# Adaptive-norm projections split over four 32-column groups of TensorE's array, in a fused two-layer decoder step

## The reference, cut to what matters

```python
cs = jax.nn.silu(c)                                   # 9 x 1024
for li in range(DEPTH):                               # DEPTH = 2
    mod = cs @ ada_w[li] + ada_b[li]                  # 9 x 3072
    shift, scale, gate = jnp.split(mod, 3, axis=-1)
    h = rmsnorm(x, norm_g[li]) * (1.0 + scale[:, None]) + shift[:, None]
    ...                                               # y = pool_branch(h) or gla_branch(h)
    x = x + gate[:, None] * y
return rmsnorm(x, final_g), ...
```

## Time and profile before

| | |
|---|---|
| median of 3 runs | 1827.49 us (1827.28 to 1830.14) |
| span of the profiled execution (first to last instruction) | 1825.0 us |
| TensorE busy with matmuls | 1747.8 us, 96% of the span |
| VectorE, ScalarE, GpSimd busy | 794.3, 509.7, 403.2 us |
| the 96 matmul records of line 1429 (layer 0's projections) | 592 ns each |
| the 384 records of line 1463 (layer 1's) | 273 ns each |

### The profile page before, as it was taken

The page is one execution under the profiler, slowest core; times in us unless marked ns, Lnnn a source line. Parts: engine busy times, 40 slices in busy tenths (PEclk is TensorE's granted clock), DMA queues, the critical chain, the costliest instruction groups (busy, mean ns, idle before and its releaser), DMA issues.

```text
span 1825.0 us, 26848 instructions
## 1 busy us (share of the span) xinstructions
PE 1747.8 (96%) x10405; PEld 1609.0 (88%) x10405; DVE 794.3 (44%) x1211; ACT 509.7 (28%) x1085; POOL 403.2 (22%) x404
## 2 busy tenths in 40 slices
PE   7899999999999999996999999999999999999997
PEld 4299999999999999994798799997999989999896
DVE  1655345634663466347113362133621336313365
ACT  5511111111111112115315322253222542124422
POOL 1222121212121212113214212142121331123310
PEclk9999999999999999998999999999999999999999
DMA  9222221221122122201111211112111121111212
GB/s 336 88 62 61 70 60 52 61 70 54 59 61 70 51 62 61 70 13 25 42 40 48 87 48 36 47 37 92 53 36 47 36 93 41 47 47 35 87 47 98
DMA packets 145141, 115.17 MB, mean 63 GB/s; under 512 B 5597, under 2 KB 127865, under 8 KB 145026
## 3 DMA queue, kind: packets, MB, share of 16 engines
q1 hardware_dynamic: 143402, 112.86, 19.9%
q10 hardware_dynamic: 1632, 0.65, 0.2%
HBM read 98.95 MB, written 15.00 MB: 62 GB/s over the span
## 4 chain that ended last, share of the span: by engine, by line
PE 89%; DVE 6%; ACT 2%; issue 2%; POOL 1%; ACTq 0%; DVEq 0%; POOLq 0%
PE psA L454 44%; PE psB L454 29%; PE psB L1623 2%; PE psX L1463 2%; PE psB L1573 2%; PE psB L1590 2%; PE psX L1555 1%; PE psX L1612 1%; PE psB L1581 1%; DVE PQ L385 1%; DVE h_lo L376 1%; PE psX L1429 1%; PE psB L351 1%; DVE y_rows L1380 1%; DVE a_hi L525 1%
## 5 line engine op out<-in xcount | busy, mean ns | idle before, releaser
L305 POOL TENSOR_TENSOR w_lo<-stage,w_hi 128x1024 fp32r<-128x1024 f32 x112 | 278.7, 2489 | 1081.9 <-ACT w_hi L300 1081.9
L454 PE MATMUL psA<-h_hi,w_hi 128*128 128x362 f32 (+1 forms) x1152 | 278.0, 350 | 13.0 <-POOL w_lo L305 6.1
L454 PE MATMUL psA<-h_lo,w_hi 128*128 128x362 f32 (+1 forms) x1152 | 256.1, 331 | 0.0
L454 PE MATMUL psA<-h_hi,w_lo 128*128 128x362 f32 (+1 forms) x1152 | 255.0, 330 | 0.0
L454 PEld LDWEIGHTS psA<-h_hi,w_hi 128*128 128x128 f32 x1152 | 199.9, 192 | 58.4 <-issue 51.1
L300 ACT ACTIVATE w_hi<-stage 128x1024 fp32r<-128x1024 f32 x112 | 119.8, 1071 | 314.7 <-PE psB L454 228.2
L454 PEld LDWEIGHTS psA<-h_lo,w_hi 128*128 128x128 f32 x1152 | 203.1, 191 | 0.0
L454 PEld LDWEIGHTS psA<-h_hi,w_lo 128*128 128x128 f32 x1152 | 202.6, 191 | 0.0
L454 PE MATMUL psB<-h_hi,w_hi 128*128 128x362 f32 (+1 forms) x576 | 128.2, 330 | 2.2 <-ACT kT L936 2.2
L454 PE MATMUL psB<-h_lo,w_hi 128*128 128x362 f32 (+1 forms) x576 | 126.3, 327 | 0.0
L454 PE MATMUL psB<-h_hi,w_lo 128*128 128x362 f32 (+1 forms) x576 | 125.9, 327 | 0.0
(11 more groups left out here) (261 smaller groups left out, 2498.8 us busy)
## 6 DMA issues: line engine op xcount, KB each, us to landing
stage<-in_gla_w_in SPq DMA_DIRECT2D x40, 512.0 KB, 3.8
stage<-in_pool_w_in SPq DMA_DIRECT2D x32, 512.0 KB, 4.0
ada_stage<-in_ada_w SPq DMA_DIRECT2D x24, 512.0 KB, 3.8
ada<-in_ada_w SPq DMA_DIRECT2D x4, 2048.0 KB, 21.4
stage<-in_pool_w_out SPq DMA_DIRECT2D x16, 512.0 KB, 3.5
v<-in_state_gla SPq DMA_DIRECT2D x32, 256.0 KB, 2.6
out_new_gla_sample<-v SPq DMA_DIRECT2D x32, 256.0 KB, 2.0
stage<-in_gla_w_out SPq DMA_DIRECT2D x16, 512.0 KB, 3.6
```

The source lines that it names most:

```text
L305: nc.gpsimd.tensor_tensor(w_lo[:, j % 2, :], stage[:, j % 2, :], w_hi[:, j % 2, :].bitcast(f32), ALU.subtract).then_inc(lay.lo_done, 1)
L454: last = nc.tensor.matmul(ps[u][:, t, 0:width], weight(w[:, p, :], k), a[:, k, n0:n0 + width], start=(k == 0 and pas == 0), stop=(k == kt ...
```

## The change

The eight contraction tiles of a projection no longer all go to columns 0 to 8 of the array. Tile k uses column group k % 4, and so writes to PSUM partitions 32(k % 4) to 32(k % 4) + 31; the stationary operand is 32 columns wide, 9 of them the wanted ones, the others those of the next tile, whose results nobody uses. Each group sums two tiles (k and k + 4). ScalarE copies all 128 partitions. The turn is now a matmul with `sel`, a 128 x 9 matrix of zeros and ones, which adds the four partial sums and turns them in one step. GpSimd makes `sel`, and clears `csT`, whose last 23 columns are read but not written otherwise.

```diff
+CG = 32
-        csT = sb("csT", [P, KD, NC_])
-        mod_row = sb("mod_row", [NC_, P], stack=early)
+        mod_row = sb("mod_row", [P, P], stack=early)
+        csT = sb("csT", [P, KD * NC_ + CG - NC_], stack=early)
+        sel = sb("sel", [P, NC_], stack=early)
...
             link(pool.memset(eps[:], EPS))
+            link(pool.memset(csT[:], 0.0))
+            link(pool.memset(sel[:], 0.0))
+            for j in range(4):
+                link(pool.affine_select(out=sel[:], in_=sel[:], compare_op=ALU.not_equal, fill=1.0, base=-CG * j,
+                                        pattern=[[-1, NC_]], channel_multiplier=1))
             pool.memset(gs_tmp[:], 0.0).then_inc(consts_ready, 1)
...
-                nc.scalar.activation(mod_rows[:, i * 512:(i + 1) * 512], X[i % 2][0:NC_, :], ACT.Copy)\
+                nc.scalar.activation(mod_rows[:, i * 512:(i + 1) * 512], X[i % 2], ACT.Copy)\
...
-                    last = nc.tensor.transpose(ps[0][:, i // 2, c:c + NC_],
-                                               mod_rows[:, i * 512 + m * P:i * 512 + (m + 1) * P],
-                                               ident[0:NC_, 0:NC_])
+                    last = nc.tensor.matmul(ps[0][:, i // 2, c:c + NC_],
+                                            mod_rows[:, i * 512 + m * P:i * 512 + (m + 1) * P], sel[:],
+                                            start=True, stop=True)
...
-                    last = nc.tensor.matmul(X[i % 2][0:NC_, :], csT[:, k, :], src[:, k, :], start=(k == 0),
-                                            stop=(k == KD - 1))
+                    rows = slice(CG * (k % 4), CG * (k % 4) + CG)
+                    last = nc.tensor.matmul(X[i % 2][rows, :], csT[:, k * NC_:k * NC_ + CG], src[:, k, :], start=(k < 4),
+                                            stop=(k >= 4))
```

In the loop the same is done to `ada_mini` (line 1463, streamed operand `ada_stage`, output `X[1][rows, P:2 * P]`), to `ada_turn` (line 1455) and to ScalarE's copy into `mod_row` (line 878):

```diff
-                    return nc.tensor.transpose(X[1][:, 2 * P:2 * P + NC_], mod_row[:], ident[0:NC_, 0:NC_])
+                    return nc.tensor.matmul(X[1][:, 2 * P:2 * P + NC_], mod_row[:], sel[:], start=True, stop=True)
```

More of the change, by code:

```diff
@@ L204, in trunk @@
         c_rows = stage[0:NC_, 1, :]
-        mod_rows = oT[0:NC_].rearrange("p k t -> p (k t)")[:, 0:3 * D]
+        mod_rows = oT[:].rearrange("p k t -> p (k t)")[:, 0:3 * D]
         glT = PQ[:, 2 * T:2 * T + NT[0][1]]
@@ L820, in _ @@
             act.wait_ge(cT_done, 1)
-            nc.scalar.activation(csT[:].rearrange("p k c -> p (k c)"), X[0][:, 0:KD * NC_], ACT.Silu).then_inc(cs_ready, 1)
+            nc.scalar.activation(csT[:, 0:KD * NC_], X[0][:, 0:KD * NC_], ACT.Silu).then_inc(cs_ready, 1)
             act.wait_ge(vT_done, 1)
@@ L877, in ada_row @@
                         ada_out(a - 1)
-                    nc.scalar.activation(mod_row[:], X[1][0:NC_, P:2 * P], ACT.Copy).then_inc(mini_free, 1)
+                    nc.scalar.activation(mod_row[:], X[1][:, P:2 * P], ACT.Copy).then_inc(mini_free, 1)
                 def ada_out(a):
@@ L1462, in ada_mini @@
                     for k in range(KD):
-                        last = nc.tensor.matmul(X[1][0:NC_, P:2 * P], csT[:, k, :], ada_stage[:, k, :], start=(k == 0),
-                                                stop=(k == KD - 1))
+                        rows = slice(CG * (k % 4), CG * (k % 4) + CG)
+                        last = nc.tensor.matmul(X[1][rows, P:2 * P], csT[:, k * NC_:k * NC_ + CG], ada_stage[:, k, :], start=(k < 4),
+                                                stop=(k >= 4))
                     last.then_inc(mini_done, 1)
```

## The result

| | before | after |
|---|---|---|
| median of the runs timed together | 1827.51 us | 1798.11 us (1797.44 to 1800.01) |
| ratio to before, 95% interval | | 0.9835 [0.9823, 0.9847] |
| span of the profiled execution | 1825.0 us | 1795.5 us |
| first start of line 454 (after: 456) in the loop | 92.6 us | 89.2 us |

The change takes 29.4 us off the runs and 29.5 off the profiled span; forecast were 28.3. Lines move: 454 is now 456, 1429 is 1437, 1418 is 1425, 1463 is 1472, 1455 is 1463, 834 is 841, 1110 is 1117, 528 is 530.

The account below looks back on a forecast made before the run. TensorE was taken to bound the kernel (89% of the span); loop projections −26.0, turns +1.4 and head −3.7 sum to −28.3 us, giving a span of 1796.7 and runs of 1799.2 us, range 1795 to 1816.

Parts of the forecast that it names:

- constants at the start: Before TensorE's first instruction: GpSimd's two memsets and four selects delay all of the head by 1.4 us (1.0 to 1.8).
- head in all, constants included: Ahead of the pool loop: faster projections, less losses to slow clock and other engines, bring the last addition 3.7 us forward.
- 20 loop projections: Pool loop: five of six projections in each of four rounds gain 1.30 us each, −26.0 us in all.
- slot 9's four: Pool loop, between Z3 and O01: the projection's gain turns into waiting for VectorE's a_lo, so it counts 0.
- turns in slots 6 to 8: Pool loop: the turn as a product with sel takes 0.12 us more each, 12 times, +1.4 us.
- turns in slots 1 and 10: Pool loop: turns between 128-row instructions save two mode changes for one more pass, 0 in all.
- Overlap of the groups: Projections: four column groups run side by side, so a loop projection takes four rounds of 0.11, 0.44 us instead of 1.74.
- Rival 1: Projections: groups take turns in pairs under in-order issue, a loop projection gains only 0.76 us; 1813.7 us, chance 0.26.
- rival 3: Projections: column groups don't overlap, turns and constants stay as cost; 1833.0 us, or 1849.8 with drains; chance 0.11.
- Five of six slots: Pool loop: the projections in slots 0 and 5 to 8 count in full, the one in slot 9 not.
- Rival 2: Pool loop: cover is thinner, slot 0's gain meets pooling or w_lo is late; at worst +5.2, 1804.4 us; chance 0.08.
- Turns in the loop: Pool loop, 24 turns: each becomes a product with sel of two passes 0.11 us apart; +1.4 us in all.

Follow-up runs that it names:

- blocked: Changed kernel with contraction tiles sent to the column groups in the order 0,0,1,1,2,2,3,3 instead of 0,1,2,3,0,1,2,3: 1798.36 us, ratio 0.9837.
- slot 9 four times over: Changed kernel with the projection behind slot 9 of each pool round running its eight matmuls four times over: 1802.48 us, ratio 0.9857 to the kernel before.
- slots 8 and 0: Two kernels: the changed kernel with the projection behind slot 8, or behind slot 0, of each round run four times over: 1805.79 us each, ratios 0.9884 and 0.9877.
- head23x3: Changed kernel with projections 2 and 3 of the head run three times over: 1810.97 us, ratio 0.9911 to the kernel before.
- pad128: Changed kernel with 32 tiny unused matmuls (128 TensorE instructions) behind head projection 3, ahead of the pool loop: 1811.82 us, ratio 0.9906.
- twos: Changed kernel with contraction tiles sent to the column groups in the order 0,1,0,1,2,3,2,3: 1800.35 us, ratio 0.9846.

## Why the prediction was right, point by point

| term | predicted | measured (spans) |
|---|---|---|
| constants at the start | +1.4 (1.0 to 1.8) | +1.9 (10.43 to 12.31) |
| head in all, constants included | −3.7 | −3.4 (92.57 to 89.19) |
| 20 loop projections | −26.0 (1.30 each) | −25.4 (1.27 each) |
| slot 9's four | 0 | 0 (wait 0.8 to 6.0) |
| turns in slots 6 to 8 | +1.4 (0.12 each) | −0.4 (0.03 less each) |
| turns in slots 1 and 10 | 0 | −0.8 (0.105 less each), of which slot 1 gave +0.4 back |
| the first jump back | not foreseen | +0.5 |
| layer 1 | 0 (not touched) | −0.4 |
| sum | −28.3 | −29.5 |

The terms of the head and the pool loop sum to −29.1, and by VectorE's instructions the changed kernel is 29.1 us ahead at the end of the pool loop. The other 0.4 arises in layer 1, where the distance wanders between 28.4 and 30.8, most at the wait for `ksm`.

**Overlap of the groups.** Right, and by the row on which it rested: the row groups of the earlier trace rows. Rounds of 0.11 us were forecast and are there (109 ns from the second round to the third and on to the fourth). The gain is 1.27 and not 1.30: the first round took 133 ns, and the four starts of a round lie 20 ns apart. The Trainium skill (TensorE: Matmul & The Clock Gate, Part 3) would have matmuls start and end strictly in program order. The trace disagrees: in blocked the four passes that start within 40 ns can only be of four groups (one group starts a pass each 0.11 us, and the gaps of 3.3 ns for each pass between say the same), so they start ahead of passes that stand before them in the program. Rival 1 fell with it, rival 3 too, and the whole −29 against +6 hangs on this one step.

**Five of six slots.** Right. Slot 9's gain turned into a wait of the predicted size (1.5 us, forecast 1.4), and slot 9 four times over cost the loop nothing. Rival 2 doubted slot 0: giving its gain back cost 5.5 us in the loop, so it had gained in full.

**Turns in the loop.** The term that was mis-sized. I took a pass 0.11 us behind the last, from the earlier trace rows, and still paid for the change of mode ahead of the projection. The row of 115.95 holds two passes in 0.28, of which each is 0.25: they start 28 ns apart (25 to 28 in all 24 turns). Between the last product and the projection lie 0.38 us against 0.41: 0.17, 0.03 and 0.19, where I had 0.165, 0.11 and 0.25. The earlier trace rows show pairs that follow each other; a single pair doesn't pay that pace (why was not tried). In the head, where 16 passes come in a row, the pace of 0.12 holds (1.95). The turns in slots 1 and 10, which I had at nothing, take 0.305 us from the product ahead to the matmul behind, where they took 0.41. Slot 10's four keep that (−0.4). Slot 1's four don't: the wait of line 1458 for ScalarE's `G` behind them grew from 0.17 to 0.30 us (2.0 to 2.5 in all).

**Constants.** Too low by 0.5: the six instructions took 1.88, with a pause of 0.26 in the middle of the four selects (10.22 to 12.10 on GpSimd).

**Head.** Each addition came 0.3 to 0.45 us after its forecast (47.4, 65.1, 83.5), which is the constants' error. The two losses on the way, from −7.6 to −4.9 by the slow clock in turns 2 and 3 and from −4.9 to −3.4 in turn 5, came as forecast: 3.58 us for 3.6, and 1.88 for 1.8.

The agreement of the sum (28.3 for 29.5) is helped by errors that cancel, which is luck: −1.8 in the turns of slots 6 to 8, −0.4 in slot 10's, +0.5 in the jump, +0.6 in the projections, +0.3 in the head, −0.4 in layer 1, whose code is the same.

## What to carry to other kernels

A float32 product whose stationary operand has few columns is bound by passes, not by work: split over four column groups it went 4.4 times as fast from first start to last (0.37 against 1.64 us), and row groups in the same trace had told so. Take slot by slot what each gain turns into: one of six was given back to VectorE here, and in the head 10 us became 3.4 because ScalarE's queue and a slowed clock stood behind. And when an edit changes the number of instructions ahead of or in a loop, count the instruction packets on the page first: in this study three more of them, one for each jump back, came with 2 to 14 us that were not the work of the edit (slots 8 and 0 about 2, slot 9 4.4, head23x3 and pad128 13 to 14, the lower clock behind the gaps included).

## What the runs showed of the hardware that I had not expected

- Passes of four column groups start 6 to 7 ns apart, and a group's waiting passes do not hold up the others; the starts come 3.3 ns apart for each pass of the program that lies between (blocked, twos).
- The two passes of one tiny float32 matmul start 25 to 28 ns apart where it stands alone between other matmuls, 0.12 us where such matmuls follow each other.
- A jump back leaves TensorE 0.5 to 1.4 us without work, and up to 2.4 us more where, as I read the packets, a 16 KB block of instructions ends just behind the target: 0, 64, 128 and 192 instructions ahead of the loop gave 1798.1, 1798.3, 1811.8 and 1798.7 us.
- Behind the empty 2.2 us of such a stall the granted clock of the next 3.8 us was 0.56, and this cost nearly as much again as the stall (pad128).
- Behind one and the same wait of 1.68 us, once in each head of layer 1, the next two matmuls took anything from 1.1 to 2.0 us; around the 2.0 of slot 9's second head the granted clock was 0.78, around the 1.2 of the changed kernel's it was 0.88. Profiles of two kernels can differ by 1 to 2 us by this alone.
